# Block 2's neighbourhood attention: value weights of heads 4 and 5 in split f32r form, their turns and mixes half a panel later, and VectorE's head work ahead of the rotary parts

## What is computed

```python
D_MODEL = 1024; SEQ = 256; NA_HEADS = 8; NB_HEADS = 8; NB_KV_HEADS = 2; HEAD_DIM = 64
# second_block, between its two SwiGLU parts
    u = rms_norm_2(h, mix_norm[l])
    z = u @ w_in[l]
    qa, ka, va, qb, kb, vb, ga, gb = jnp.split(z, SPLITS, axis=-1)
    ya = neighbourhood_attention_2d(qa, ka, va, na_rpb[l])
    qb = rope(qb.reshape(B, T, NB_HEADS, HEAD_DIM), pos)
    kb = rope(kb.reshape(B, T, NB_KV_HEADS, HEAD_DIM), pos)
    yb = windowed_gqa_sink(qb, kb, vb, sink_logit[l])
    merged = jax.nn.sigmoid(ga) * (ya @ w_branch_a[l]) + jax.nn.sigmoid(gb) * (yb @ w_branch_b[l])
    h = h + merged @ w_out[l]
# neighbourhood_attention_2d, for one row of the grid
    s = jnp.einsum('bchd,bicjhd->bhcij', q_r, k_g).astype(jnp.float32) * scale
    s = s + bias[None]
    p = jax.nn.softmax(s.reshape(B, H, GRID_W, kh * NA_KW), axis=-1)
    return jnp.einsum('bhcij,bicjhd->bchd', p, v_g)
```

## Time and profile before

| | |
|---|---|
| median of 3 runs | 952.65 us (952.59 to 952.65) |
| profiled execution | 952.4 us, its span 950.5 us |
| granted TensorE clock, mean | 0.999 |
| PE busy | 943.2 us (99%), 5400 matmuls |
| DVE busy | 665.9 us (70%) |
| ACT busy | 536.3 us (56%) |
| POOL busy | 62.3 us (7%) |
| DMA | 173.14 MB, mean 182 GB/s |

### The profile page before, as it was taken

The page is one execution under the profiler, slowest core; times in us unless marked ns, Lnnn a source line. Parts: engine busy times, 40 slices in busy tenths (PEclk is TensorE's granted clock), DMA queues, the critical chain, the costliest instruction groups (busy, mean ns, idle before and its releaser), DMA issues.

```text
span 950.5 us, 13952 instructions
## 1 busy us (share of the span) xinstructions
PE 943.2 (99%) x5400; PEld 826.7 (87%) x5400; DVE 665.9 (70%) x857; ACT 536.3 (56%) x691; POOL 62.3 (7%) x95
## 2 busy tenths in 40 slices
PE   9999999999999999999999999999999999999997
PEld 8999988888888888898888888999888898888886
DVE  7888869876655565688666666878887586665665
ACT  7687688535444444474454445679674465444544
POOL 1200000002000000022221000100100020000000
PEclk9999999999999999999999999999999999999999
DMA  9785335553756555547666655545435555655541
GB/s 304 227 244 168 110 123 182 199 178 118 273 181 197 199 177 184 187 160 243 207 207 204 201 177 177 181 137 170 133 133 178 177 192 185 220 178 183 194 153 44
DMA packets 119471, 173.14 MB, mean 182 GB/s; under 512 B 3168, under 2 KB 91488, under 8 KB 119424
## 3 DMA queue, kind: packets, MB, share of 16 engines
q1 hardware_dynamic: 117904, 168.41, 54.9%
q0 software_dynamic: 1376, 3.81, 1.4%
q10 hardware_dynamic: 144, 0.26, 0.1%
HBM read 171.42 MB, written 1.05 MB: 181 GB/s over the span
## 4 chain that ended last, share of the span: by engine, by line
PE 99%; DVE 0%; ACT 0%; issue 0%
PE pair L726 22%; PE pair L729 11%; PE acc L695 10%; PE acc L697 10%; PE acc L696 10%; PE pair L695 6%; PE pair L697 6%; PE pair L696 6%; PE pair L713 2%; PE pair L717 2%; PE pair L714 2%; PE acc L1065 1%; PE pair L923 1%; PE acc L1214 1%; PE acc L853 1%; PE pair L871 1%
## 5 line engine op out<-in xcount | busy, mean ns | idle before, releaser
L726 PE MATMUL pair<-actp,wh 128*128 128x512 f32 x912 | 292.8, 396 | 0.0
L1806 DVE TENSOR_TENSOR wl<-raw,wh 128x2048 fp32r<-128x2048 f32 x89 | 204.8, 2303 | 62.7 <-ACT wh L1338 62.7
L1338 ACT ACTIVATE wh<-raw 128x2048 fp32r<-128x2048 f32 x88 | 168.3, 1913 | 84.1 <-PE acc L697 84.1
L729 PEld LDWEIGHTS pair<-actp,wl 128*128 128x128 f32 x912 | 171.3, 188 | 40.0
L729 PE MATMUL pair<-actp,wl 128*128 128x256 f32 x912 | 179.2, 278 | 0.0
L1802 DVE TENSOR_TENSOR wl<-raw,wh 128x2048 fp32r<-128x2048 f32 x68 | 155.6, 2291 | 31.3 <-ACT wh L1332 30.9
L1332 ACT ACTIVATE wh<-raw 128x2048 fp32r<-128x2048 f32 x69 | 132.1, 1916 | 70.9 <-PE pair L697 27.4
L726 PEld LDWEIGHTS pair<-actp,wh 128*128 128x128 f32 x912 | 141.6, 189 | 1.4
L1553 ACT ACTIVATE arena<-pair 128x512 f32<-128x512 f32 x57 | 34.1, 598 | 170.8 <-PE pair L726 170.8
L695 PE MATMUL acc<-wh,midh 128*128 128x512 f32 x310 | 120.9, 390 | 0.0
L697 PE MATMUL acc<-wh,midl 128*128 128x512 f32 x310 | 120.6, 389 | 0.0
(11 more groups left out here) (375 smaller groups left out, 1452.3 us busy)
## 6 DMA issues: line engine op xcount, KB each, us to landing
raw<-in_w_in SPq DMA_DIRECT2D x35, 1024.0 KB, 5.2
raw<-in_mlp_w SPq DMA_DIRECT2D x32, 1024.0 KB, 5.2
raw<-in_ffn_w_gate SPq DMA_DIRECT2D x22, 1024.0 KB, 5.4
raw<-in_ffn_w_up SPq DMA_DIRECT2D x22, 1024.0 KB, 5.4
raw<-in_ffn_w_down SPq DMA_DIRECT2D x22, 1024.0 KB, 5.0
raw<-in_w_out SPq DMA_DIRECT2D x8, 1024.0 KB, 4.9
raw<-in_w_up_rnn SPq DMA_DIRECT2D x4, 1024.0 KB, 5.2
raw<-in_w_in SPq DMA_DIRECT2D x5, 512.0 KB, 5.5
```

Of the source, the lines that this page charges most:

```text
L726: return nc.tensor.matmul(bank[:, :].rearrange("p (u t) -> p u t", u=2), h[:, k, cs], actp[:, :, k, :], **kw)
L729: return nc.tensor.matmul(bank[:, 0:T], l[:, k, cs], acth[:, k, :], **kw)
L1338: nc.scalar.activation(wh[:, slot(n), :], raw[:, slot(n), :], ACT.Copy).then_inc(hi_ready, 1)
L1806: nc.vector.tensor_tensor(wl[:, slot(n), :], raw[:, slot(n), :], wh[:, slot(n), :].bitcast(F32), ALU.subtract).then_inc(lo_ready, 1)
```

## The change

Heads 4 and 5 go over to the second form: FV is 4 in place of 6. Their value parts get places of their own: `vn4`, high and low part of head 4, one tile of keys in the unused tail of wh and one in that of wl, and `vn5` for head 5, a new tile; ScalarE and DVE write them in panel VA2 + 3 in three more operations each. `y2` takes the result of the two heads, the transposes of L1296 and their waits go, and `out_hi`/`out_lo` of that pair read y2. To make room, hid and kcd move into `arena`. The turns of heads 4 and 5 go from places 15 and 17 to 16 and 18, their mixes from 17 and 19 to 18 and 20. And on DVE the head steps of a panel's middle come ahead of the rotary parts and the key split (`heads2(n, 0)` moves up), which changes the order in the panels QB + 1 and QB + 2. Line numbers of the kernel after differ a little; L1233 there is L1229 here, L1218 is L1214.

```diff
-        hid = sb("hid", [P, 2, 2, 2 * NC])
...
+        hid = carve(15392, 2, 2, 2 * NC)
+        kcd = carve(15512, GR, 2 * NC)
...
+        y2 = carve(14592, T)
+        vn5 = sb("vn5", [P, TT, P], F32R)
+        vn4 = [v[:, R * PW:R * PW + P] for v in (wh_all, wl_all)]
...
-        FV = 6
+        FV = 4
...
-        turn_at = places((7, 9, 11, 13, 15, 17, 20, 22, 23, 25, 26, 27, 28, 30, 31, 32))
-        mix_at = places((9, 11, 13, 15, 17, 19, 21, 23, 25, 26, 27, 28, 29, 31, 32, 33))
+        turn_at = places((7, 9, 11, 13, 16, 18, 20, 22, 23, 25, 26, 27, 28, 30, 31, 32))
+        mix_at = places((9, 11, 13, 15, 18, 20, 21, 23, 25, 26, 27, 28, 29, 31, 32, 33))
...
-                if n == GA2 + 3:
-                    pe.wait_ge(normed, NH + FV)
-                    pe.wait_ge(midl_ready, 2)
-                    for tt in range(TT):
-                        m = nc.tensor.transpose(ps[OUT_A][:, tt * P:(tt + 1) * P], atok2[:, tt, 2 * P:3 * P], ident)
-                    m.then_inc(atok_turned, 1)
...
+                    for kt in range(TT):
+                        nc.scalar.activation(vn4[kt][:, 0:DH], va[:, kt, DH * 4:DH * 5], ACT.Copy)
+                    nc.scalar.activation(vn5[:, :, 0:DH], va[:, :, DH * 5:DH * 6], ACT.Copy)
...
-                    to = y3 if k < NH else ybT[:, (k - NH) // 2, :]
+                    to = (y2, y3)[k // 2 - 2] if k < NH else ybT[:, (k - NH) // 2, :]
...
                     rope(kbT[:, :], swk, rope1[:, 0:T], rope2[:, 0:T], T, 1).then_inc(kb_roped, 1)
+                heads2(n, 0)
                 if n - 1 in (QB, QB + 1):
...
                     m.then_inc(kst_ready, 1)
-                heads2(n, 0)
                 if n - 1 in (QB + 1, QB + 2):
```

More of the change, by code:

```diff
@@ L177, in build @@
         pcT = carve(8224, 4, P)
-        kcd = sb("kcd", [P, GR, 2 * NC])
+        hid = carve(15392, 2, 2, 2 * NC)
+        kcd = carve(15512, GR, 2 * NC)
         thr = sb("thr", [P, T])
@@ L650, in head2 @@
                         [va[:, kt, DH * h:DH * (h + 1)] for kt in range(TT)] if h < FV else
-                        [vns[:, kt, h - FV, :, :].rearrange("p s d -> p (s d)") for kt in range(TT)])
+                        vn4 if h == 4 else [vn5[:, kt, :] for kt in range(TT)] if h == 5 else
+                        [vns[:, kt, h - 6, :, :].rearrange("p s d -> p (s d)") for kt in range(TT)])
             g = h // 4
@@ L1729, in _ @@
                     act.wait_ge(va_evac, 2)
-                    nc.scalar.activation(vns[:, :, :, 0, :], va[:, :, DH * FV:DH * NH].rearrange("p k (h d) -> p k h d", h=2),
+                    for kt in range(TT):
+                        nc.scalar.activation(vn4[kt][:, 0:DH], va[:, kt, DH * 4:DH * 5], ACT.Copy)
+                    nc.scalar.activation(vn5[:, :, 0:DH], va[:, :, DH * 5:DH * 6], ACT.Copy)
+                    nc.scalar.activation(vns[:, :, :, 0, :], va[:, :, DH * 6:DH * NH].rearrange("p k (h d) -> p k h d", h=2),
                                          ACT.Copy).then_inc(vnh_ready, 1)
@@ L1754, in _ @@
                     else:
-                        act.wait_ge(atok_turned, 3)
-                        nc.scalar.activation(midh[:, 2, :], ps[OUT_A][:, 0:T], ACT.Copy)
                         act.wait_ge(normed, 2 * NH)
+                        nc.scalar.activation(midh[:, 2, :], y2, ACT.Copy)
                         nc.scalar.activation(midh[:, 3, :], y3, ACT.Copy).then_inc(midh_ready, 1)
@@ L2402, in _ @@
                     dve.wait_ge(vnh_ready, 1)
-                    nc.vector.tensor_tensor(vns[:, :, :, 1, :], va[:, :, DH * FV:DH * NH].rearrange("p k (h d) -> p k h d", h=2),
+                    for kt in range(TT):
+                        nc.vector.tensor_tensor(vn4[kt][:, DH:P], va[:, kt, DH * 4:DH * 5], vn4[kt][:, 0:DH].bitcast(F32), ALU.subtract)
+                    nc.vector.tensor_tensor(vn5[:, :, DH:P], va[:, :, DH * 5:DH * 6], vn5[:, :, 0:DH].bitcast(F32), ALU.subtract)
+                    nc.vector.tensor_tensor(vns[:, :, :, 1, :], va[:, :, DH * 6:DH * NH].rearrange("p k (h d) -> p k h d", h=2),
                                             vns[:, :, :, 0, :].bitcast(F32), ALU.subtract).then_inc(vn_ready, 1)
@@ L2413, in _ @@
                         dve.wait_ge(midh_ready, 3)
-                        nc.vector.tensor_tensor(midl[:, 2, :], ps[OUT_A][:, 0:T], midh[:, 2, :].bitcast(F32), ALU.subtract)
+                        nc.vector.tensor_tensor(midl[:, 2, :], y2, midh[:, 2, :].bitcast(F32), ALU.subtract)
                         nc.vector.tensor_tensor(midl[:, 3, :], y3, midh[:, 3, :].bitcast(F32), ALU.subtract).then_inc(midl_ready, 1)
```

## The result

| | before | after |
|---|---|---|
| median | 952.59 us (5 runs, 952.48 to 952.65) | 959.31 us (5 runs, 958.75 to 959.69) |
| ratio, 95% interval | | 1.007 (1.0059 to 1.0081) |
| profiled execution, its span | 952.4, 950.5 us | 958.75, 957.0 us |
| granted TensorE clock, mean | 0.999 | 0.996 |

The kernel after is 6.7 us slower. The direction was forecast, with 957.0 us; the time is 2.3 us above that, at the very end of the range (959.31 for an end of 959.3). The chain that the forecast follows is there, link by link. What it left out of its sum is there too: the fall of the clock, rival 3.

What follows compares the result with a forecast made beforehand. TensorE, 99% busy, was taken to bound the kernel, with DVE becoming late: +4.3 us at head 6's mix, -0.2 for L1296, +0.3 later waits, together +4.4, median 957.0 us; range 955.0 to 959.3 us.

Steps and rivals of the forecast that it cites:

- The chain that the forecast follows: ScalarE and DVE steps in block 2, from 652.9 to 672.5, delaying the mix of head 6 by 4.3 us.
- rival 3: Clock falls during TensorE's long wait ahead of head 6's mix; about 2.2 us more, 959.2 us; chance 0.10.
- TensorE's own work: Heads 4 and 5 mixes in f32r save 0.70 us, two L1296 transposes 0.18: 0.9 us less on TensorE.
- The first copy: ScalarE's copy of head 4's turn, behind head 5's exponentials, ends at about 652.9; DVE's low part waits for it.
- The second copy: ScalarE's copy of head 5's turn, behind the second query swap, ends at 663.5; DVE waits from 661.8.
- Norm of head 5: On DVE, at the end of its row of work, ends at 672.5; TensorE's mix of head 6 waits for it.
- The waits of TensorE: About 4 us ahead of head 6's mix, 0.7 at head 5's mix, 0.2 at head 6's turn; together 5.
- The bound of 5% of the chain: The 19.6 us from 652.9 to 672.5 may be off 5%, 1 us either way: 956.0 to 958.1 us.
- Later short waits, +0.3: Behind head 6's mix, head 7's mix and turn follow DVE closely: 0 to 0.5 us more, taken as 0.3.
- Both reasons against it: Against a clock fall at head 6's mix: a mix and a turn split the pause, and TensorE was full before it.
- Rivals 1 and 2: One DVE wait for ScalarE does not arise, 955.2 us, chance 0.07; or DVE keeps up, not slower, chance 0.08.
- rival 2: DVE keeps up at head 6's mix, so not slower; with both DVE waits gone 953.2 us; chance 0.08.

Runs made afterwards that it cites:

- the run with the places alone: Kernel before with only the new turn and mix places of heads 4 and 5, still plain f32, old DVE order: 956.18 us.
- the run with the filled wait: Kernel after with 16 unused matmuls of 512 columns into a free bank ahead of the mix of head 6: 957.6 us.
- the run with VectorE's old order: Kernel after with DVE's head steps of a panel's middle put back behind the rotary parts and key split: 953.63 us.
- the form alone: Kernel after with heads 4 and 5 in f32r form, but turns and mixes at old places and old DVE order: 960.12 us.

## Why the prediction came out as it did, step by step

- **TensorE's own work**: right (0.75 us won up to the turn of head 6, as just shown, for the 0.70 of the two mixes). The f32r mix of head 4 takes 656.72 to 657.20, 0.48 us, as forecast; 10 matmuls fewer on the page (5390, has 5400).
- **The first copy** was forecast to end at 652.9: 653.14. **The rotary parts** at 656.2: the key parts behind them start at 656.43. **The low weights** at 661.8: 662.09. **The second copy** at 663.5: 663.94. **Norm of head 4** at 664.5: 664.99. **Norm of head 5** at 672.5: 673.20. **Mix of head 6** at 672.6: 673.25. The two waits of VectorE for ScalarE were 2.29 and 1.89 us, forecast as 1.9 and 1.7, and the swap of the second query pair came 2.58 us later than in before, forecast as 2.4.
- **The waits of TensorE**: 4.07 us, forecast about 4; 0.81, forecast 0.7; the turn of head 6 comes 0.73 us behind the mix of head 5, where 0.48 is usual, so 0.25 for the forecast 0.2.
- **The bound of 5% of the chain** held: its end, 673.20, is 0.7 us later than forecast. Of that 0.18 is no error of the chain: ScalarE's swap with which it starts stands at 648.57 here and at 648.39 in before, and TensorE, too, is 0.16 later by the start of block 2 (its first weight matmul at 592.31, before 592.15), ahead of all that was changed there. The other 0.5 grew link by link, some 0.05 to 0.2 each; which hand-over costs them wasn't tried.
- **Later short waits, +0.3**: they did not come. The mix of head 8 is 6.59 us later than in before (689.09 and 682.50), that of head 15 6.36 (719.84 and 713.48), and between them lie the 0.23 us of L1296. Behind the turn of head 7 next to nothing was lost.
- **The step that failed: the clock left out of the sum** (rival 3, with a chance of 0.10). Both reasons against it were wrong. The mix and the turn that were to split the pause stand ahead of it, beside the 0.81 us of head 5, and from the end of the panel's last matmul to 673.25 it is 4.07 us without a break. And TensorE was full ahead of the single pause of 2.06 us in the run with the places alone, which did not protect it. A fall could have been seen in before: the windows there give a granted clock of 0.75 from 948 to 949 us and 0.50 from 949 to 950, behind the last matmul, which starts at 944.22. The price of 2.2 us, taken from the start of the program, was too high: it is 1.64 us in the trace and 1.7 us in the run with the filled wait. The row it was taken from does not show a clock either: the windows of before give 1.00 over those 14 matmuls, and in the trace of after the same 14 take 4.89 us, not 5.9. The Trainium skill ("TensorE: Matmul & The Clock Gate", Part 1, The HAM clock gate) says that an idle TensorE falls back to 1.2 GHz and that activity releases it; the trace agrees (0.50 behind the pause of 4.07 us, 1.00 again in the windows from 678 on), and the forecast should have followed it.

The sum as it was: the mix of head 6 later by 4.8 (673.25 - 668.28, less the 0.16 of the start), the clock 1.64, L1296 -0.23, together 6.2; with the 0.16 of the start 6.4 of the 6.5 us between the two spans. Forecast were 4.3, nothing, -0.2 and 0.3. Rival 3's time of 959.2 is so near to the 959.31 by luck: its clock was 0.6 too dear and its later waits 0.3, against a chain 0.7 too short and a profiled execution that lies 0.56 us under the median (958.75), where 0.25 was taken over.

Rivals 1 and 2 did not occur here, but the run with VectorE's old order is rival 2's picture: both waits for ScalarE gone, the norm of head 5 at 669.20 (the prediction reckoned with 668.9 for that case) and 953.6 us (953.2).

## What to carry to other kernels

A wait that is put earlier in an engine's queue takes with it all that is queued behind; here the rotary and key parts, 3.6 us of work whose input was there, stood behind one that had to wait for ScalarE, and a ring through the other engine made the delay come back a panel later. Ask for each operation that is moved up not whether it is wanted sooner, but whether its input is there. And where TensorE was never idle, reckon with the clock for a new pause of about 2 us or more: in the profiled executions the stretch behind the mix of head 6 became 1.5 to 2.6 us longer (1.69 us for the pauses of 2.06 and 2.64, 1.46 for 3.40, 1.64 for 4.07, 2.58 for 5.49).

## What the runs showed of the hardware

In the profiled executions the clock's fall depended on the pause as follows. After single pauses of 1.0, 1.1 and 1.4 us the granted clock stayed at 1.00; after 2.06, 2.64, 3.40, 4.07, 5.49 and 5.86 us it went to 0.50. I had expected that a pause near 2 us passes. The fall need not come in the pause: behind 2.06 us it came 1.6 us after TensorE had gone back to work, while in the form alone, with the pause of 5.86 us, it stood at 0.64 on average over the idle five microseconds themselves:

```profile
655.00:660.00 5.00, 0.00 (x0) 0.00 (x0) 4.86 (x11) 2.26 (x3) 0.00 (x0) 0.64 0.56 179
660.00:665.00 5.00, 4.64 (x19) 4.11 (x20) 2.13 (x9) 3.62 (x7) 0.00 (x0) 0.68 0.08 31
```

So part of the slow time fell where it cost nothing, and the price does not simply grow with the pause. Between 1.4 and 2.06 us no pause was tried. And it is not the same in every execution of one kernel: with the places alone, three of six executions have the time and the mean clock of a kernel without a fall.
